# Squared-ReLU MLPs by seven products: sums and halves of the weight quarters at the ends of a group's first part, and a slab's low half in two GpSimd operations

## The reference, cut to what matters

```python
def _mlp(h, w1, w2):
    return jnp.square(jax.nn.relu(h @ w1)) @ w2

for i in range(DEPTH):                       # DEPTH = 2
    ...                                      # x = x + mixer(_rmsnorm(x, ...))
    x = x + _mlp(_rmsnorm(x, norm_mlp[i]), w_mlp1[i], w_mlp2[i])
return _rmsnorm(x, norm_final)
```

## Time and profile before

| | us |
|---|---|
| median of 3 runs (lowest, highest) | 1213.17 (1210.65, 1214.13) |
| the profiled execution, its own time | 1212.27 |
| its span in the trace | 1210.4 |
| outside the span | 1.9 |
| TensorE busy | 1149.8 |
| VectorE busy | 866.5 |
| ScalarE busy | 583.9 |
| GpSimd busy | 406.4 |

### The profile page before, as it was taken

The page is one execution under the profiler, slowest core; times in us unless marked ns, Lnnn a source line. Parts: engine busy times, 40 slices in busy tenths (PEclk is TensorE's granted clock), DMA queues, the critical chain, the costliest instruction groups (busy, mean ns, idle before and its releaser), DMA issues.

```text
span 1210.4 us, 17086 instructions
## 1 busy us (share of the span) xinstructions
PE 1149.8 (95%) x6469; PEld 981.2 (81%) x6469; DVE 866.5 (72%) x1358; ACT 583.9 (48%) x1042; POOL 406.4 (34%) x219
## 2 busy tenths in 40 slices
PE   7999988999999999999997899989999999999997
PEld 5788877878988979988765778878789889799886
DVE  5866698678579488565569798747786785894654
ACT  6677666545244254234373377854452451452333
POOL 2433322431131141146643375324411311402441
PEclk9999989999999999999998999999999999999999
DMA  5233331531421421143322100105414315221332
GB/s 159 73 109 94 98 114 40 156 110 48 174 70 61 148 82 57 41 141 104 74 67 70 35 19 27 45 18 158 120 53 155 89 35 175 70 70 35 98 95 87
DMA packets 154377, 105.15 MB, mean 87 GB/s; under 512 B 9062, under 2 KB 138385, under 8 KB 154306
## 3 DMA queue, kind: packets, MB, share of 16 engines
q1 hardware_dynamic: 153036, 104.09, 28.4%
q10 hardware_dynamic: 1270, 0.13, 0.1%
HBM read 102.04 MB, written 6.35 MB: 90 GB/s over the span
## 4 chain that ended last, share of the span: by engine, by line
PE 65%; DVE 22%; ACT 6%; issue 4%; POOL 1%; DMA 1%; SPq 0%; DVEq 0%; ACTq 0%
PE bank L780 19%; PE bank L782 19%; PE bank L781 19%; PE bank L984 3%; DVE tbuf L2149 3%; DVE probs L2112 2%; DVE tbuf L2152 2%; ACT ur L1286 2%; DVE mask_c L2137 2%; DVE ur L1950 2%; DVE xhl L2173 1%; ACT wh L1286 1%; DVE xhl L2166 1%; POOL wl L1772 1%; PE bank L996 1%
## 5 line engine op out<-in xcount | busy, mean ns | idle before, releaser
L1772 POOL TENSOR_TENSOR wl<-raw,wh 128x1024 fp32r<-128x1024 f32 x123 | 301.2, 2452 | 666.0 <-ACT wh L1286 666.0
L780 PE MATMUL bank<-ur,wh 128*128 128x512 f32 (+1 forms) x784 | 298.1, 380 | 12.0 <-POOL wl L1772 12.0
L782 PE MATMUL bank<-ur,wl 128*128 128x512 f32 (+1 forms) x784 | 295.5, 377 | 0.0
L781 PE MATMUL bank<-ur,wh 128*128 128x512 f32 x688 | 268.5, 390 | 0.0
L1286 ACT ACTIVATE wh<-raw 128x1024 fp32r<-128x1024 f32 x123 | 128.7, 1052 | 265.3 <-PE bank L782 261.6
L780 PEld LDWEIGHTS bank<-ur,wh 128*128 128x128 f32 x784 | 147.9, 189 | 44.5 <-issue 18.6
L782 PEld LDWEIGHTS bank<-ur,wl 128*128 128x128 f32 x784 | 147.8, 189 | 27.1
L781 PEld LDWEIGHTS bank<-ur,wh 128*128 128x128 f32 x688 | 129.4, 188 | 26.4 <-issue 0.5
L781 PE MATMUL bank<-xhl,wh 128*128 128x512 f32 (+2 forms) x392 | 145.4, 371 | 0.0
L780 PE MATMUL bank<-xhl,wh 128*128 128x512 f32 (+1 forms) x296 | 123.7, 418 | 7.6 <-POOL xhl L1772 3.0
L1286 ACT ACTIVATE ur<-tbuf 128x512 fp32r<-128x512 f32 (+2 forms) x116 | 67.5, 585 | 114.1 <-DVE tbuf L2149 44.6
(11 more groups left out here) (259 smaller groups left out, 2310.0 us busy)
## 6 DMA issues: line engine op xcount, KB each, us to landing
raw<-in_w_mlp SPq DMA_DIRECT2D x80, 512.0 KB, 3.8
raw<-in_w_in_e SPq DMA_DIRECT2D x18, 512.0 KB, 3.6
probs<-in_w_mlp SPq DMA_DIRECT2D x12, 512.0 KB, 4.9
rstd_qk<-in_w_mlp SPq DMA_DIRECT2D x12, 512.0 KB, 3.8
sq<-in_w_mlp SPq DMA_DIRECT2D x12, 512.0 KB, 4.9
raw<-in_w_in_o SPq DMA_DIRECT2D x10, 512.0 KB, 3.7
raw<-in_w_out_e SPq DMA_DIRECT2D x8, 512.0 KB, 4.1
raw<-in_w_out_o SPq DMA_DIRECT2D x8, 512.0 KB, 3.7
```

Source lines behind the costliest of these rows:

```text
L780: mm(dst, lhs[0], rhs[0], start=start, stop=False, skip_group_check=not check)
L781: mm(dst, lhs[0], rhs[1], start=False, stop=False, skip_group_check=not check)
L782: return mm(dst, lhs[1], rhs[0], start=False, stop=stop, skip_group_check=not check)
L1772: return nc.gpsimd.tensor_tensor(dst, a, b, ALU.subtract)
```

## The change

1. **Second and third group.** ScalarE rounds quarter x for the next group (product 0's weights) behind the last rounding of the group before, once product 5 has ended; VectorE makes the low halves ahead of its last `product_added`. At the group's start, before slab 0 has ended, ScalarE rounds product 1's weights and VectorE makes their sums (y - x) and low halves. Between slabs only the two sums for slot 2 remain, both behind slab 6.
2. **First group.** ScalarE rounds x right behind the norm's root. VectorE makes x's low halves and the two sums before it takes slab 0. Product 1's weights are rounded behind slabs 1 and 3, their low halves made behind slabs 2 and 4.
3. **Odd slabs 1, 3, 5.** The pair A12, A22 is rounded first, then S1, then S2 and S4 (`second_combos`); slab 7 puts it last. VectorE waits for all three sums before the first of its subtractions.
4. **GpSimd** makes a slab's low half in two operations of 512 columns in the loop of `mlp`, 64 slabs in all (24 of layer 0, 40 of layer 1); `w_lo` is counted by the second.
5. In the second part, product 0's result is added before the sums for product 4's quarter, not between them.

```diff
+        def second_combos(j):
+            first, second, sums = (t.rearrange("p (c t) -> p c t", t=HS) for t in (u_first, u_second, u_sums))
+            straight, summed = (A12, A22, second, 0), [(S1, S1, first[:, 2:3, :], 2), (S2, S4, sums, 4)]
+            return [straight] + summed if j < 3 else summed + [straight]
...
@@ ScalarE, fast_group
+                if g == 0:
+                    act.wait_ge(slab_done, base)
+                    quarter_rounded(G, 0)
+                else:
+                    act.wait_ge(product_done, BANKS_DONE * G)
+                    quarter_rounded(G, 1)
                 for s in range(KT):
...
-                    if s in (0, 1):
-                        quarter_rounded(G, 0, (s,))
-                    if s in (3, 5):
-                        quarter_rounded(G, 1, (s // 5,))
+                    if g == 0 and s in (1, 3):
+                        quarter_rounded(G, 1, (s // 3,))
...
                 quarter_rounded(G, 6)
+                if g + 1 < FAST:
+                    act.wait_ge(product_done, BANKS_DONE * G + 12)
+                    quarter_rounded(G + 1, 0)
...
@@ GpSimd, mlp
-                        split((n0 + s) % 2, KT * g + (n0 + s))
+                        slot = (n0 + s) % 2
+                        pool.wait_ge(w_hi, KT * g + (n0 + s + 1))
+                        sub(wl[:, slot, 0:512], raw[:, slot, 0:512], wh[:, slot, 0:512].bitcast(F32))
+                        sub(wl[:, slot, 512:1024], raw[:, slot, 512:1024], wh[:, slot, 512:1024].bitcast(F32)).then_inc(w_lo, 1)
...
@@ VectorE, fast_group
+                if g == 0:
+                    quarter_low(G, 0, 0)
+                    quarter_low(G, 0, 1)
+                quarter_sum(G, 0, 0)
+                quarter_sum(G, 0, 1)
+                if g:
+                    quarter_low(G, 1, 0)
+                    quarter_low(G, 1, 1)
                 for s in range(KT):
...
-                    if s in (1, 2):
-                        quarter_low(G, 0, s - 1)
-                    if s == 3:
-                        quarter_sum(G, 0, 1)
                     if s == 6:
-                        quarter_low(G, 1, 1)
+                        quarter_sum(G, 1, 0)
...
-                    if s == 2:
-                        quarter_sum(G, 0, 0)
-                    if s == 4:
-                        quarter_low(G, 1, 0)
+                    if g == 0 and s in (2, 4):
+                        quarter_low(G, 1, s // 4)
                     if s == 6:
-                        quarter_sum(G, 1, 0)
+                        quarter_sum(G, 1, 1)
...
-                quarter_sum(G, 1, 1)
...
+                if g + 1 < FAST:
+                    quarter_low(G + 1, 0, 0)
+                    quarter_low(G + 1, 0, 1)
                 product_added(G, 6)
```

More of the change, by code:

```diff
@@ L1438, in fast_group @@
                         nc.scalar.activation(u_second, u_scaled, ACT.Square).then_inc(u_ready, 1)
[L1439 to L1444, removed]
-                    if s in (0, 1):
-                        quarter_rounded(G, 0, (s,))
-                    if s in (3, 5):
-                        quarter_rounded(G, 1, (s // 5,))
+                        for c0, c1, src, made in second_combos(j):
+                            if made:
+                                act.wait_ge(sums_made, SUMS * G + 4 * j + made)
+                            else:
+                                act.wait_ge(u_ready, u + s + 1)
+                            copy(combo_h[:, c0:c1 + 1, j, :], src).then_inc(combo_hi, 1)
+                    if g == 0 and s in (1, 3):
+                        quarter_rounded(G, 1, (s // 3,))
                 act.wait_ge(slab_done, base + KT)
@@ L2168, in fast_group @@
                     else:
-                        for k, (c0, c1, src) in enumerate(((S1, S1, first[:, 2:3, :]), (S2, S4, sums), (A12, A22, second))):
+                        dve.wait_ge(sums_made, SUMS * G + 4 * j + 4)
+                        for k, (c0, c1, src, _) in enumerate(second_combos(j)):
                             dve.wait_ge(combo_hi, done + k + 2)
-                            if k == 1:
-                                dve.wait_ge(sums_made, SUMS * G + 4 * j + 4)
                             v.tensor_tensor(combo_l[:, c0:c1 + 1, j, :], src, f(combo_h[:, c0:c1 + 1, j, :]),
                                             ALU.subtract).then_inc(combo_lo, 1)
-                quarter_sum(G, 1, 1)
                 quarter_low(G, 2, 0)
                 quarter_low(G, 2, 1)
+                product_added(G, 0)
                 quarter_sum(G, 2, 0)
-                product_added(G, 0)
                 quarter_sum(G, 2, 1)
```

## The result

The changed kernel took **1204.81 us** (median of 4, 1203.93 to 1205.4), against 1213.49 (1210.65 to 1214.13) for the kernel before on the same chip: ratio 0.9934, 95% interval 0.9918 to 0.995. The forecast was 1206.5 in 1203.5 to 1210.8. Its profiled execution spans 1202.5 us, 7.9 less than before.

What follows compares the result with a forecast made beforehand. TensorE is busy for 95% of the span, so only its idle time can be won. Terms: -7.9 - 1.7 + 2.2 + 1.0 = -6.4 us, giving 1205.9 from the profiled execution or 1206.8 from the median; forecast 1206.5, range 1203.5 to 1210.8.

Steps and rivals of the forecast that it cites:

- Second and third groups: Both layers' MLPs: TensorE's stops ahead of slabs 4 and 6 go, -1.97 us in each of four groups, -7.9 in all.
- The norm: The wait for the norm's last square goes as VectorE gets between GpSimd's halves: 0.85 us a layer, -1.7 in all.
- The first groups: First group of each layer's MLP: 3.5 + 0.7 - 3.1 = +1.1 us a layer, +2.2 in all, clock apart.
- The stop: First group, ahead of slab 3: TensorE stops for 3.5 us where it had not stopped.
- The +0.7 at slab 4: First group: a further TensorE stop of 0.7 us, with slab 4 due at 266.8 and GpSimd ending about 267.4.
- 3.1: First group: the old losses of 1.61, 1.27 and 0.24 us that go, 3.1 a layer.
- The clock: TensorE's clock may fall after the first group's stop, costing nothing to 2.7 us a layer; taken as +1.0 in one layer.
- better case: First stop shorter than reckoned, time below 1205 us; chance 0.07.
- Rival 1: GpSimd keeps the ports over both halves, so the norm's wait stays (+1.7 us): about 1207.6 us; chance 0.13.
- Rival 2: The clock falls after the first group's stop in both layers and stays low, +4.4 us: 1210.9 us; chance 0.12.
- Rival 3: Moved work is late at the group's start and delays the chain; both stops back, +7.9 us: 1214.4 us; chance 0.07.
- Rival 4: GpSimd's second half waits each time for a whole VectorE operation, +16.8 us over slabs 2 to 7: 1223 us; chance 0.04.

Runs made afterwards that it cites:

- e1_whole: The changed kernel with GpSimd's low half of a slab again in one operation of 1024 columns: 1205.62 us, ratio 0.9943 to the kernel before.
- e5 to e8: Four variants of the changed kernel, each placing the first group's quarter work elsewhere: 1197.11, 1191.89, 1198.71 and 1200.53 us.
- e3_old_pairs: The changed kernel with the combinations of slabs 1, 3 and 5 again in their old order: 1204.75 us, ratio 0.9939 to the kernel before.
- e4_moved: The kernel before with only the quarters' work moved, GpSimd's operation whole and combinations in old order: 1206.15 us, ratio 0.9947.
- e5_gap_all: The changed kernel with the first group's two low halves of x and two sums ahead of VectorE's copy of the norm's factors: 1197.11 us, ratio 0.9874.
- e6_gap_lows: The changed kernel with the first group's low halves in VectorE's wait for the spreading matmul, its sums behind slab 0's and 1's differences: 1191.89 us, ratio 0.9830.
- e2_halves: The kernel before with one edit, GpSimd's low half in two operations of 512 columns: 1210.70 us, ratio 0.9988.

## Why the prediction was right

- **Second and third groups: right, and too small.** Predicted -1.97 a group, measured -2.49, so -10.0 in place of -7.9. I had counted the two stops only. Before, 0.27 was also missing at product 0's first matmul, and the last 0.25 in steps below 0.1 each, the largest two right behind the stops. The first went with the late VectorE work, the others with the stops. Comparing the piece with 192 pitches would have given 2.51 at once. The chain itself fits: shifted by the 1.78 us by which the group starts later, slab 4's rounding was predicted at 348.2 (measured 348.19), GpSimd's start at 349.3 (349.32), its end at 352.1 (352.04).
- **The norm: right, and too small.** The wait of 0.85 idle went, and 0.25 a layer of slower restart with it that the sum had left out: -2.2 in place of -1.7. VectorE's square got in between GpSimd's two halves. e1_whole shows the halves are the cause. The pair took 2.98 with the square beside it.
- **The first groups: right in the sum, not in its terms.** With the 1.05 us by which this execution was late there, slab 0 was predicted to be taken at 256.05 (256.05), slab 3 rounded at 258.45 (258.44), GpSimd to start at 259.55 (259.55). The stop was 3.43 idle for 3.5 (the prediction's own terms give 261.3 - 257.9 = 3.4). The +0.7 at slab 4 did not show because slab 3 ran at the lower clock and took longer; in e1_whole's layer 0, without a fall, it was 0.69. And more than 3.1 went: product 0's first matmul had been 0.40 late by the step, where 0.24 idle was counted, and some 0.4 stood in small steps. So apart from the clock the first groups came out even, where +2.2 was forecast. e5 to e8 show that VectorE's order is what sets this stop.
- **The clock: the mechanism right, the count not.** A fall was put at +1.0 in one layer; there was one of 3.4 us in both, each worth 1.6 (below) and hiding the 0.7 at slab 4. The first groups were to lose 3.2 in all with it and lost 3.3: the clock took 2.2 more than forecast and the rest 2.1 less. That these two errors cancel is luck.
- **The rest.** The seven products of a group took 40.31 or 40.32 us after and 40.39 to 40.42 before, -0.6 in all, counted at nothing. -10.0 - 2.2 + 3.3 - 0.6 = -9.5, against a span shorter by 7.9: the remaining +1.6 lies outside the MLPs. 1.3 of it stands in front of the first group, and was there by 24 us, long before any instruction that the change touched: ScalarE's rounding that started at 22.23 before starts at 23.62, and the first fall of the clock came at 20.0 us in place of 15.5. The other 0.3 is in layer 1's mixer: a fall near 798 us, absent before, cost 1.6, and one near 647 us, shorter by half, gave back 1.1. So the span's -7.9 against the forecast's -6.4 is -3.2 in the three terms that were too small, +0.1 in the first groups and +1.6 of this. The time, 1204.81, lies in the band that the prediction kept for its better case (below 1205, a chance of 0.07), but not for that case's reason: the first stop was no shorter than reckoned.
- **The rivals.** Rival 1 is out (square 1.37 long). Rival 2's mechanism is real: falls of 6.8 us came in one layer of e1_whole and of e3_old_pairs and in both of e4_moved, where the piece was 0.8 to 1.5 longer than in the changed kernel, whose two falls were short. Rival 3 is out. Rival 4's mechanism, GpSimd standing behind VectorE, was seen in e5_gap_all (4.26 for a half), but only behind a row of long operations, and between slabs there is none.

The clock's price is the plainest in the first groups. In TensorE's timeline of the changed kernel the starts behind the stop lie 0.43 apart in place of 0.23:

```profile
262.92 0.63 PE L787 MATMUL bank<-ur,wh 128*128 128x512 f32 x1
263.35 0.63 PE L788 MATMUL bank<-ur,wl 128*128 128x512 f32 x1
...
265.86 0.39 PE L788 MATMUL bank<-ur,wl 128*128 128x512 f32 x1
```

The eight steps from 262.37 to 265.86 take 3.49 us where eight pitches are 1.81. Of the 1.68 between, 0.08 comes behind every stop, also where the clock stays up, so the fall costs 1.6: about half of its 3.4 us. Without a fall the stops alone make the piece: 36.03 (e6_gap_lows, without a stop) and stops of 3.26 + 0.69 are 39.98, as measured in e1_whole's layer 0.

The forecast also missed what this work could bring: VectorE is idle ahead of `rstd` (3.19 us in the row above), and two of the four operations fit in there for nothing. That is worth 5 us a layer, more than the stop itself, since the fall of the clock goes too.

## What to carry to other kernels

Compare a whole stage with its count of matmuls times the pitch before adding up its visible stops; the small steps below the eye's threshold were a fifth of the gain here. When work is moved ahead of the first consumer of a chain, look for the nearest idle time of that engine further up, here the wait for a matmul's result, and put only as much there as fits: two operations cost nothing, four shut GpSimd out for 3 us. A stop of some 3 us on TensorE costs its length and then, where the clock falls behind it as it did in seven of eight cases here, about half of the low stretch.

## What was not expected of the hardware

- **The two engines take turns at the shared ports, but not always.** Between two back-to-back GpSimd operations a waiting VectorE operation gets in (first sum 1.10 us, square 1.37). The other way round it holds too in most cases. In the changed kernel, first group, GpSimd's second half gets in between a difference and a low half that VectorE runs back to back, so the low half takes 2.31 in place of 1.22:

```profile
265.60 2.72 POOL L1785 TENSOR_TENSOR wl<-raw,wh 128x512 fp32r<-128x512 f32 x2 [3.38 <-ACT wh L1292]
...
266.07 1.10 DVE L2169 TENSOR_TENSOR tbuf<-tbuf 128x256 f32<-128x256 f32 x1 [0.84 <-ACT tbuf L1445]
267.10 2.31 DVE L1966 TENSOR_TENSOR probT_h<-probs,w_late_h 128x1024 fp32r<-128x1024 f32 x1
```

The exception is e5_gap_all, in both layers: with two more VectorE operations of 1024 columns to come in a row, GpSimd's 1.2 us took 4.26 and 4.28. The Trainium skill (SBUF — State Buffer, Who interferes with whom) has each holding the ports for a whole instruction; these traces agree with that. What made GpSimd miss its turn in that row is open.
- **Two GpSimd halves cost 2.52 to 2.56 us alone**, 2.72 with one VectorE operation of 256 columns between them, 2.98 with one of 512, and 3.13 or 3.22 in e2_halves with one of 256 and the last 0.6 us of one of 1024 ahead of them; the whole operation takes 2.39 alone. The split is worth it only where VectorE's wait is on the path.
- **The same stop is not always followed by the same clock.** After an idle of 3.11 the clock stayed up once and was low for 6.8 us in the other layer of the same execution (e1_whole). After 3.10 it was low for 6.8 us twice (e4_moved), after 3.42 or 3.43 for 3.4 us three times and for 6.8 once (the changed kernel, e3_old_pairs). After 1.03 to 1.47 it never fell in these groups.
